# ScalarE's copies of the turned probabilities, moved ahead of a weight slot's high part in the attention steps

## The chip, the cores and the metric

The kernel runs on one core of one Trainium2 chip. The metric is the device time of one execution in microseconds (us), as a median over runs. Five engines of the core have instruction streams of their own: TensorE (PE in the profile, with PEld for its weight loads), VectorE (DVE), ScalarE (ACT), GpSimd (POOL) and SyncE (SP), which issues the weight transfers. Each stream is written out by hand, and semaphores tie them together.

## What is computed

Two transformer stacks run one after the other on one sequence of 256 tokens and width 1024, with float32 inputs. The change lies in the first stack, whose two layers each do this, cut to what matters:

```python
h = h + 0.5 * swiglu(rmsnorm(h, g0), ...)            # d_ff 2816
u = rmsnorm(h, g1)
cols = u @ w_in[l]                                   # projections of four mixers
y_a = mla_mixer(...)    # 8 heads, dense causal
y_b = swa_mixer(...)    # 8 heads, window 128, with sinks
y_c = nsa_mixer(...)    # 8 heads: compressed, selected and window attention
y_d = diff_mixer(...)   # 4 heads, difference of two softmaxes
merged = sum(sigmoid(u @ w_gate[l, b]) * (y_b_ @ w_branch[l, b]) for b in range(4))
h = h + merged @ w_o[l]
h = h + 0.5 * swiglu(rmsnorm(h, g2), ...)
```

The second stack (dilated attention, then retention, each between two feed-forward blocks) is not touched.

## The kernel before, in words

**Weights.** All weights come as a stream of slots of 128x3072 float32 (1.5 MB) into a ring in SBUF. A product of full precision is made from two parts of each operand, a high part (the value rounded to fp32r) and a low part (the rest). For a slot, ScalarE writes the high part (`take_high`, line L1579, tile `ring_hi`, two buffers), VectorE subtracts it from the slot to get the low part (`take_low`, L1961, tile `ring_lo`), and TensorE then multiplies with both. `take_high` waits until the slot has landed (`weights_in`) and until TensorE has done with the slot that last used the same `ring_hi` buffer (`ring_used`).

**The attention of a layer** is one loop of 22 steps on every engine, `for t in range(STEPS)`. It does three things interleaved: the softmax attention of 20 pairs of heads, the small compression network of the third mixer (`compress`), and the projections and gated merges that fill TensorE's time. In step t TensorE does, in this order:

- `scores(t)`: the scores of pair t (banks 0 and 1 of PSUM);
- `turn(t)`: it transposes the probabilities of pair t-1 into banks 2 and 3 (L1175; six matmuls for a pair of two jobs, three in steps 9 to 12, whose pairs are differential heads with one job);
- two pieces, number 2t and 2t+1: a projection `tile` for numbers below 12, and a `merge` from number 12 (step 6) on. A merge multiplies a gate's weights (24 matmuls) and, for most, a branch's (12 matmuls) from the slot of that step;
- `values(t-1)`: the turned probabilities of pair t-1 times the values.

A merge writes into one of two PSUM banks, and so waits until VectorE has emptied the bank of the merge two numbers before (semaphore `merged`, in `merge`, by `merge_emptied`).

**VectorE** does in step t: `empty(2t-1)` (scales the gate of piece 2t-1 into `gate_in`, L2601), `bias_max(t)` (L2507 to L2513), `add(2t-1)` (`add_branch`: L2616 for the first branch, L2618 and L2620 for the others; it waits for ScalarE's tanh of the gate), `take_low` of the slot, `normalise(t)` (L2523 to L2542), `empty(2t)`, `low_outputs`, `compress(t)`, `add(2t)`. Within it, step 3 gives `cmp_kv_out` (L2461), for which TensorE's `turn(4)` waits; step 5 gives `cmp_shifted` (L2478), for which `turn(6)` waits; the end of step 14 is `low_diff` of step 14 (L2566), for which `turn(15)` waits.

**ScalarE** does in step t: `compress(t)`, `take_high` of the slot, `copy_pT(t-1)` (L1846: it copies the turned probabilities from banks 2 and 3 to SBUF, once for each job, and waits for TensorE's `turn(t)` by `probs_turned`), the tanh of gate 2t-1 (`gate`, L1851), `exps(t)` (L1834, L1835), `copy_outputs` (L1860), and the tanh of gate 2t. Every step's slot is listed in `SPLIT_STEPS` (steps 0, 2, 3 and 5 to 20). In steps 0, 2 and 20 (`LATE_SPLITS`) `take_high` stands behind `exps`; in the other 16 it stands where the change is.

The three streams share no scheduler: the order of the calls in the source is the order on the engine.

Of the kernel before, what the change touches and what calls it, by code (L numbers as in the profile page):

```python
# [174 lines left out]
def build(nc, stream, x_rows, norm_gT_2, gains_2, table_2, pick_2, ret_const, decay, norm_gT, mla_gT, sinks, posT, lam, subln, table_1, consts, flip_dram, pick_1, out):  # L175

    ctx = ExitStack()
    with ctx:
# [309 lines left out]
        def mix_slot(l):  # L488
            return l * C_LAYER + C_FFN
# [102 lines left out]
        PAIRS = NU // 2  # L592

        def jobs(t):

            return 1 if UNITS[2 * t]["kind"] == "diff" else 2
# [3 lines left out]
        def jobs_before(l, t):  # L600

            return l * JOBS_LAYER + sum(jobs(n) for n in range(t))
# [99 lines left out]
        def merge_at(i):  # L702

            return i - 12 if i >= 12 else None
# [18 lines left out]
        def branches_before(m):  # L723

            return sum(merge_parts(n)[3] for n in range(m))
# [54 lines left out]
        def emptied_before(c):  # L780


            return SPLIT_SLOTS[SPLIT_INDEX[c] - 2] + 1
# [788 lines left out]
        def _(act):  # L1572

            def take_high(c):

                act.wait_ge(weights_in[c % NS], 16 * (c // NS + 1))
                if SPLIT_INDEX[c] >= 2:
                    act.wait_ge(ring_used, emptied_before(c))
                act.activation(split_part(c, high(c)), split_part(c, ring[:, c % NS, :]), ACT.Copy)\  # L1579
                    .then_inc(hi_ready, 1)  # L1580
# [75 lines left out]
            def take_high_late(c):  # L1656


                act.wait_ge(weights_in[c % NS], 16 * (c // NS + 1))
                act.activation(high(c)[:, 0:2 * D], ring[:, c % NS, 0:2 * D], ACT.Copy).then_inc(hi_ready, 1)  # L1660

            def take_high_unused(c):


                act.wait_ge(weights_in[c % NS], 16 * (c // NS + 1))
                act.activation(high(c)[:, 2 * D:], ring[:, c % NS, 2 * D:], ACT.Copy).then_inc(hi_back, 1)
# [151 lines left out]
            def compress(l, t):  # L1818
                if t == 3:
                    act.wait_ge(cmp_taken, 2 * l + 2)  # L1820
                    act.activation(hidC[:, :, :], hidC[:, :, :], ACT.Gelu_apprx_tanh).then_inc(cmp_gelu, 1)
                elif t == 6:
                    act.wait_ge(cmp_shifted, l + 1)
                    act.activation(ce[:, :, :, :], cs[:, :, :, :], ACT.Exp).then_inc(cmp_exp, 1)

            def exps(l, t):
                if t or l:
                    act.wait_ge(probs_turned, jobs_before(l, t))
                s = pair_soft(l, t)
                for j, u in enumerate(UNITS[2 * t:2 * t + 2]):  # L1830
                    a = l * NU + 2 * t + j
                    x, p = biased_sb[:, j, :], probs_sb[:, j, :]
                    act.wait_ge(negmax_ready, a + 1)
                    act.activation(p[:, 0:P], x[:, 0:P], ACT.Exp, bias=s[:, 1, j, 0:1], accum_out=s[:, 2, j, 0:1])  # L1834
                    last = act.activation(p[:, P:3 * P], x[:, P:3 * P], ACT.Exp, bias=s[:, 1, j, 1:2],  # L1835
                                          accum_out=s[:, 2, j, 1:2])
                    if u["kind"] == "swa":
                        last = act.activation(s[:, 3, j, :], s[:, 1, j, :], ACT.Exp, bias=sink[:, l, u["head"]:u["head"] + 1])
                    last.then_inc(exp_done, 1)

            def copy_pT(l, t):
                for j in range(jobs(t)):
                    act.wait_ge(probs_turned, jobs_before(l, t) + j + 1)
                    if l or t:
                        act.wait_ge(attn_out, jobs_before(l, t))
                    act.activation(pT_sb[:, j, :], ps[:, 2 + j, 0:3 * P], ACT.Copy).then_inc(pT_ready, 1)  # L1846

            def gate(l, m):
                g = gates_before(m)
                act.wait_ge(gate_scaled, 32 * l + g + 1)  # L1850
                act.activation(gate_place(m), gate_in[:, g % 2, :], ACT.Tanh, scale=0.5).then_inc(sig_ready, 1)  # L1851

            def copy_outputs(l, t):


                if branch_copy(t) is None:
                    return
                dst, src = branch_copy(t)
                act.wait_ge(attn_out, jobs_before(l, t + 1))
                act.activation(dst.rearrange("p f t -> p (f t)"), src, ACT.Copy).then_inc(branch_in, 1)  # L1860

            def copy_diff(l):
                for fp in range(2):
                    act.wait_ge(diff_turned, 2 * l + fp + 1)
                    act.activation(yT[0][:, 2 * fp:2 * fp + 2, :].rearrange("p f t -> p (f t)"), ps[:, 2 + fp, :],
                                   ACT.Copy).then_inc(branch_in, 1)

            def attention(l):
                for t in range(STEPS):
                    compress(l, t)  # L1870
                    if t in SPLIT_STEPS and t not in LATE_SPLITS:
                        take_high(mix_slot(l) + SPLIT_STEPS[t])
                    if 1 <= t <= PAIRS:
                        copy_pT(l, t - 1)
                    if t and merge_at(2 * t - 1) is not None:
                        gate(l, merge_at(2 * t - 1))
                    if t < PAIRS:
                        exps(l, t)
                    if t in SPLIT_STEPS and t in LATE_SPLITS:
                        take_high(mix_slot(l) + SPLIT_STEPS[t])  # L1880
                    if t >= 2:
                        copy_outputs(l, t - 2)
                    if t == 14:
                        copy_diff(l)
                    if merge_at(2 * t) is not None:
                        gate(l, merge_at(2 * t))
                gate(l, merge_at(2 * STEPS - 1))
                take_high(mix_slot(l) + S_BRANCH_2 + 1)
                take_high_unused(mix_slot(l) + S_WO)
                for k in range(K_SPLIT):  # L1890
                    if k == 3:
                        act.wait_ge(ring_used, emptied_before(mix_slot(l) + S_WO))
                        take_high_late(mix_slot(l) + S_WO)
                    act.wait_ge(merged, 32 * l + branches_before(32) + 1 + k)
                    act.activation(mTh[:, k, :], mT[:, k, :], ACT.Copy).then_inc(merged_hi, 1)
                take_high(mix_slot(l) + S_WO + 1)
# [8 lines left out]
            for l in range(DEPTH):  # L1905
                norm(3 * l + 0, norm_g[:, l, 0, :])
                ffn(2 * l, layer_slot(l))
                take_high_late(layer_slot(l) + C_FFN + 1)
                take_high_back(layer_slot(l) + C_FFN)
                norm(3 * l + 1, norm_g[:, l, 1, :])  # L1910
                take_high_back(layer_slot(l) + C_FFN + 1)
                act.wait_ge(r_ready, 3 * l + 2)
                projections(l)
                attention(l)
                for j in range(2):
                    take_high(layer_slot(l + 1) - C_FFN + j)
                norm(3 * l + 2, norm_g[:, l, 2, :])
                ffn(2 * l + 1, layer_slot(l + 1) - C_FFN)
                take_high_late(layer_slot(l + 1) + 1)
# [1080 lines left out]
```

## Time and profile before

| | |
|---|---|
| median of 3 runs | 2782.04 us (2781.07 to 2783.23) |
| the profiled execution | 2783.28 us, its span 2781.2 us |
| PE busy | 2733.8 us, 98% of the span |
| PEld busy | 2399.6 us, 86% |
| DVE busy | 1879.8 us, 68% |
| ACT busy | 1387.9 us, 50% |
| steps 1 to 21 of the attention, first layer | 292 to 514 us of the span |
| the same, second layer | 1003 to 1225 us |

Busy time counts an engine's instructions; an engine that waits on a semaphore isn't busy. A wait is shown in brackets behind a row of the timeline: how long the engine sat idle before the instruction, and what released it. The second layer's attention repeats the first's 711.3 us later, row for row, with differences of a few tenths.

### The profile page before, as it was taken

To read this page: it belongs to the slowest core of one execution; us is meant where nothing else is said; L and a number is where in the kernel's file an instruction comes from. 1 tells how busy PE (TensorE), PEld (TensorE's weight loads), DVE (VectorE), ACT (ScalarE), POOL (GpSimd) and SP (SyncE) were. 2 spreads that over 40 slices of the span, in tenths; PEclk is the share of its full clock that TensorE was granted. 3 is DMA by queue.
4 is the path that set the end of the run, shared out by engine and by line. 5 is a ranking of instruction groups with operands and counts; after the bars stand their busy time and mean duration, and the time that the engine had idled before them with its cause. 6 is when DMAs were issued, how large, how long until landed. Compare 5 with 4: busy or idle time off the path is not lost.

```text
span 2781.2 us, 42124 instructions
## 1 busy us (share of the span) xinstructions
PE 2733.8 (98%) x16902; PEld 2399.6 (86%) x16902; DVE 1879.8 (68%) x2840; ACT 1387.9 (50%) x1960; POOL 103.0 (4%) x131
## 2 busy tenths in 40 slices
PE   8999999999999999999999999999999999999998
PEld 7888999888888989988888889997888889987787
DVE  6676678666776657867676675555667666755766
ACT  5453455454545545545455454445455454453554
POOL 1000000000000000001001001110000000000000
PEclk9999999999999999999999999999999999999999
DMA  7554343445455543446455545453454455444453
GB/s 265 187 203 160 142 155 137 182 170 192 177 185 183 203 160 139 158 159 236 183 183 192 190 179 172 166 178 133 181 191 171 181 191 190 163 150 168 159 184 125
DMA packets 49670, 488.46 MB, mean 176 GB/s; under 512 B 6656, under 2 KB 6864, under 8 KB 11272
## 3 DMA queue, kind: packets, MB, share of 16 engines
q1 hardware_dynamic: 44200, 471.71, 45.9%
q0 software_dynamic: 5344, 14.98, 1.9%
q8 instruction: 90, 1.47, 0.2%
q14 instruction: 36, 0.29, 0.0%
HBM read 485.47 MB, written 1.19 MB: 175 GB/s over the span
## 4 chain that ended last, share of the span: by engine, by line
PE 91%; DVE 5%; ACT 1%; issue 1%; DMA 0%; POOL 0%; SPq 0%; DVEq 0%; ACTq 0%
PE ps L896 70%; PE ps L961 17%; DVE ring_lo L1961 2%; PE ps L912 1%; PE ps L1175 1%; ACT ring_hi L1579 1%; PE ps L1385 1%; PE ps L1400 1%; DVE xn L2108 0%; PE ps L1292 0%; DVE work_all L2618 0%; DVE uT L1985 0%; PE ps L1027 0%; PE ps L1082 0%; PE ps L924 0%
## 5 line engine op out<-in xcount | busy, mean ns | idle before, releaser
L896 PE MATMUL ps<-uT,ring_hi 128*128 128x512 f32 (+1 forms) x5536 | 1509.6, 344 | 4.2 <-DVE ring_lo L1989 2.6
L896 PE MATMUL ps<-uT,ring_lo 128*128 128x256 f32 x4176 | 1176.7, 282 | 0.0
L896 PEld LDWEIGHTS ps<-uT,ring_hi 128*128 128x128 f32 x5536 | 954.9, 190 | 138.7 <-DVE ring_lo L1989 3.0
L896 PEld LDWEIGHTS ps<-uT,ring_lo 128*128 128x128 f32 x4176 | 794.5, 190 | 6.2
L2074 DVE TENSOR_TENSOR ring_lo<-ring,ring_hi 128x2048 fp32r<-128x2048 f32 x160 | 366.8, 2293 | 221.1 <-ACT ring_hi L1647 221.1
L1961 DVE TENSOR_TENSOR ring_lo<-ring,ring_hi 128x3072 fp32r<-128x3072 f32 (+1 forms) x110 | 352.0, 3200 | 140.4 <-ACT ring_hi L1579 140.1
L1579 ACT ACTIVATE ring_hi<-ring 128x3072 fp32r<-128x3072 f32 (+1 forms) x110 | 290.8, 2644 | 210.0 <-PE ps L896 198.6
L1647 ACT ACTIVATE ring_hi<-ring 128x2048 fp32r<-128x2048 f32 x160 | 304.1, 1901 | 0.0
L961 PE MATMUL ps<-ring_hi,hid_hi 128*128 128x512 f32 x704 | 276.3, 392 | 0.0
L961 PE MATMUL ps<-ring_lo,hid_hi 128*128 128x512 f32 x704 | 276.1, 392 | 0.0
L961 PE MATMUL ps<-ring_hi,hid_lo 128*128 128x512 f32 x704 | 274.2, 389 | 0.0
L896 PE MATMUL ps<-ring_hi,uT 128*128 128x384 f32 (+1 forms) x1024 | 259.2, 333 | 0.2
L1637 ACT ACTIVATE work_all<-ps 128x512 f32<-128x512 f32 x168 | 100.4, 598 | 309.0 <-PE ps L896 308.3
L1640 ACT ACTIVATE work_all<-work_all 128x256 f32<-128x256 f32 x168 | 70.2, 418 | 299.6 <-DVE work_all L2062 299.6
L2025 DVE TENSOR_TENSOR ring_lo<-ring,ring_hi 128x1024 fp32r<-128x1024 f32 x176 | 214.6, 1219 | 4.2 <-ACT ring_hi L1620 4.2
L896 PEld LDWEIGHTS ps<-ring_hi,uT 128*128 128x128 f32 x1024 | 183.4, 188 | 1.2 <-issue 1.1
L1620 ACT ACTIVATE ring_hi<-ring 128x1024 fp32r<-128x1024 f32 x176 | 183.9, 1045 | 0.0
L896 PE MATMUL ps<-ring_lo,uT 128*128 128x384 f32 (+1 forms) x512 | 169.3, 331 | 0.0
L961 PEld LDWEIGHTS ps<-ring_hi,hid_hi 128*128 128x128 f32 x704 | 132.2, 188 | 31.9 <-DVE hid_lo L2069 1.2
L961 PEld LDWEIGHTS ps<-ring_hi,hid_lo 128*128 128x128 f32 x704 | 132.3, 188 | 29.1
L961 PEld LDWEIGHTS ps<-ring_lo,hid_hi 128*128 128x128 f32 x704 | 132.2, 188 | 21.0
L2059 DVE TENSOR_TENSOR work_all<-ps,work_all 128x512 f32<-128x512 f32 x168 | 115.8, 689 | 38.4 <-ACT work_all L1637 38.1
(317 smaller groups left out, 2805.3 us busy)
## 6 DMA issues: line engine op xcount, KB each, us to landing
ring<-stream_dram SPq DMA_DIRECT2D x297, 1536.0 KB, 6.3
mlaT_all<-bias_vectors POOLq DMA_DIRECT2D x32, 96.0 KB, 2.8
bias<-gains_dram POOLq DMA_DIRECT2D x5, 512.0 KB, 7.7
ring<-stream_dram SPq DMA_DIRECT2D x4, 512.0 KB, 7.7
yR<-bias_vectors POOLq DMA_DIRECT2D x1, 2048.0 KB, 13.9
mlaT_all<-bias_vectors POOLq DMA_DIRECT2D x32, 64.0 KB, 3.3
row<-ret_const_dram POOLq DMA_DIRECT2D x1, 1280.0 KB, 5.8
h<-x_rows_dram SPq DMA_DIRECT2D x2, 512.0 KB, 4.7
```

The source lines that it names most:

```text
L896: m = pe.matmul(out_, lhsT, rhs, start=start, stop=stop, **kw)
L912: last = pe.transpose(ps[:, banks[kp], j * SEQ + tt * P:j * SEQ + tt * P + P], h[:, tt, k * P:(k + 1) * P], ident)
L961: last = pe.matmul(ps[:, n, :], x, w[:, cols], start=False, stop=final and x is x_lo, skip_group_check=True)
L1579: act.activation(split_part(c, high(c)), split_part(c, ring[:, c % NS, :]), ACT.Copy)\
L1620: act.activation(high(c)[:, 2 * D:3 * D], ring[:, c % NS, 2 * D:3 * D], ACT.Copy).then_inc(down_hi, 1)
L1637: act.activation(gu_low, ps[:, 4 + 2 * (g % 2):6 + 2 * (g % 2), SEQ:2 * SEQ], ACT.Copy)\
L1640: act.activation(sil[:, g % 2, :], gu[:, g % 2, 0, :], ACT.Silu).then_inc(silu_ready, 1)
L1647: act.activation(high(c)[:, 0:2 * D], ring[:, c % NS, 0:2 * D], ACT.Copy).then_inc(hi_ready, 1)
L1961: dve.tensor_tensor(split_part(c, ring_lo[:, c % NS, :]), split_part(c, ring[:, c % NS, :]), split_part(c, high(c).bitcast(F32)), ALU.subt ...
L2025: dve.tensor_tensor(ring_lo[:, c % NS, 2 * D:3 * D], ring[:, c % NS, 2 * D:3 * D], high(c)[:, 2 * D:3 * D].bitcast(F32), ALU.subtract)
L2059: dve.tensor_tensor(gu[:, g % 2, :, :], ps[:, 4 + 2 * (g % 2):6 + 2 * (g % 2), 0:SEQ], gu_low, ALU.add).then_inc(gu_summed, 1)
L2074: dve.tensor_tensor(ring_lo[:, c % NS, 0:2 * D], ring[:, c % NS, 0:2 * D], high(c)[:, 0:2 * D].bitcast(F32), ALU.subtract).then_inc(lo_rea ...
```

## The change

In ScalarE's stream, in each step of the attention, `copy_pT(l, t - 1)` is now called ahead of `take_high`. Nothing is added or removed, and the streams of the other engines are the same.

```diff
             def attention(l):
                 for t in range(STEPS):
                     compress(l, t)
+                    if 1 <= t <= PAIRS:
+                        copy_pT(l, t - 1)
                     if t in SPLIT_STEPS and t not in LATE_SPLITS:
                         take_high(mix_slot(l) + SPLIT_STEPS[t])
-                    if 1 <= t <= PAIRS:
-                        copy_pT(l, t - 1)
                     if t and merge_at(2 * t - 1) is not None:
                         gate(l, merge_at(2 * t - 1))
```

The order changes in steps 3 and 5 to 19 of each layer, 16 steps. On ScalarE, before, from the tanh of gate 30 (end of step 15) to the tanh of gate 32 (end of step 16); L1579 is the slot's high part, L1846 the copies, L1851 a tanh:

```order
L1851 ACTIVATE gate_out<-gate_in 128x256 [waits gate_scaled]
L1579 ACTIVATE ring_hi<-ring 128x3072 [waits ring_used,weights_in_3]
L1846 ACTIVATE work_all<-ps 128x384 [waits attn_out,probs_turned] x2
L1851 ACTIVATE gate_out<-gate_in 128x256 [waits gate_scaled]
L1834 ACTIVATE work_all,soft<-xn,soft 128x128 [waits negmax_ready,probs_turned]
L1835 ACTIVATE work_all,soft<-xn,soft 128x256
L1834 ACTIVATE work_all,soft<-xn,soft 128x128 [waits negmax_ready]
```

The same piece in the changed kernel:

```order
L1851 ACTIVATE gate_out<-gate_in 128x256 [waits gate_scaled]
L1846 ACTIVATE work_all<-ps 128x384 [waits attn_out,probs_turned] x2
L1579 ACTIVATE ring_hi<-ring 128x3072 [waits ring_used,weights_in_3]
L1851 ACTIVATE gate_out<-gate_in 128x256 [waits gate_scaled]
L1834 ACTIVATE work_all,soft<-xn,soft 128x128 [waits negmax_ready,probs_turned]
L1835 ACTIVATE work_all,soft<-xn,soft 128x256
L1834 ACTIVATE work_all,soft<-xn,soft 128x128 [waits negmax_ready]
```

The two copies with their wait for `probs_turned` have passed the high part; the tanh and the exponentials stand behind both, as they did.

On ScalarE, before, in step 3, behind the Gelu of the compression network (L1821):

```order
L1821 ACTIVATE yR<-yR 128x60 [waits cmp_taken]
L1579 ACTIVATE ring_hi<-ring 128x3072 [waits ring_used,weights_in_3]
L1846 ACTIVATE work_all<-ps 128x384 [waits attn_out,probs_turned] x2
L1834 ACT_TABLE_LOAD [waits negmax_ready]
L1834 ACTIVATE work_all,soft<-xn,soft 128x128 [waits probs_turned]
```

and in the changed kernel:

```order
L1821 ACTIVATE yR<-yR 128x60 [waits cmp_taken]
L1846 ACTIVATE work_all<-ps 128x384 [waits attn_out,probs_turned] x2
L1579 ACTIVATE ring_hi<-ring 128x3072 [waits ring_used,weights_in_3]
L1834 ACT_TABLE_LOAD [waits negmax_ready]
L1834 ACTIVATE work_all,soft<-xn,soft 128x128 [waits probs_turned]
```

Here too only the two rows have changed places.

## Rows read from the trace of the kernel before

**Rows 1.** Busy time by stretches: us, busy us (instructions) of PE, PEld, DVE, ACT, POOL, clock
```profile
420.00:500.00 80.00, 78.92 (x662) 72.48 (x661) 64.26 (x168) 43.90 (x97) 1.64 (x1) 1.00 0.37 139
```

**Rows 2.** Timeline, step 17: start, duration, engine, line, instruction, [idle before, releaser]
```profile
465.02 2.77 ACT L1579 ACTIVATE ring_hi<-ring 128x3072 fp32r<-128x3072 f32 x1 [0.93 <-PE ps L896]
465.93 0.88 PE L1175 MATMUL ps<-cst,work_all 128*128 128x128 f32 x6
466.57 0.48 PE L896 MATMUL ps<-uT,ring_hi 128*128 128x256 f32 x2
467.69 0.85 ACT L1846 ACTIVATE work_all<-ps 128x384 f32<-128x384 f32 x2
468.43 0.42 ACT L1851 ACTIVATE gate_out<-gate_in 128x256 f32<-128x256 f32 x1
469.33 0.42 DVE L2620 TENSOR_TENSOR mlaT_all<-mlaT_all,work_all 128x256 f32<-128x256 f32 x1
470.94 0.40 PE L896 MATMUL ps<-uT,ring_hi 128*128 128x256 f32 x2
```

**Rows 3.** Timeline, ACT and PE, step 14: copies that wait for their turn
```profile
434.22 0.87 PE L1175 MATMUL ps<-cst,work_all 128*128 128x128 f32 x6
434.81 0.87 ACT L1846 ACTIVATE work_all<-ps 128x384 f32<-128x384 f32 x2 [0.60 <-PE ps L1175]
```

**Rows 4.** Timeline, PE and DVE, step 19: a merge that waits for its bank
```profile
488.05 0.88 PE L1175 MATMUL ps<-cst,work_all 128*128 128x128 f32 x6
491.74 0.42 DVE L2620 TENSOR_TENSOR mlaT_all<-mlaT_all,work_all 128x256 f32<-128x256 f32 x1
492.22 0.51 PE L896 MATMUL ps<-uT,ring_hi 128*128 128x256 f32 x2 [0.42 <-DVE mlaT_all L2620]
```

**Rows 5.** Timeline, step 3 and the turn of step 4
```profile
318.12 0.82 PE L1175 MATMUL ps<-cst,work_all 128*128 128x128 f32 x6
323.15 0.18 DVE L2523 RECIPROCAL soft<-soft 128x4 f32<-128x4 f32 x1 [0.35 <-ACT work_all L1835]
325.05 0.27 DVE L2461 COPY yR<-ps 15x128 f32<-15x128 f32 x1
326.93 0.88 PE L1175 MATMUL ps<-cst,work_all 128*128 128x128 f32 x6
```

**Rows 6.** Timeline, step 5 and the turn of step 6
```profile
336.31 0.87 ACT L1846 ACTIVATE work_all<-ps 128x384 f32<-128x384 f32 x2 [2.06 <-PE ps L1175]
337.45 3.35 DVE L1961 TENSOR_TENSOR ring_lo<-ring,ring_hi 128x3072 fp32r<-128x3072 f32 x1
343.78 0.41 DVE L2478 TENSOR_TENSOR yR<-yR 128x240 f32<-128x240 f32 x1
346.04 0.87 PE L1175 MATMUL ps<-cst,work_all 128*128 128x128 f32 x6
```

**Rows 7.** Timeline, end of step 7 on DVE and the turn of step 8
```profile
367.62 0.41 DVE L2616 SCALAR_TENSOR_TENSOR mlaT_all<-gate_out,ps 128x256 f32<-128x256 f32 x1
368.15 0.88 PE L1175 MATMUL ps<-cst,work_all 128*128 128x128 f32 x6
```

**Rows 8.** Timeline, step 11 and the first merge of step 12
```profile
400.54 0.55 PE L1175 MATMUL ps<-cst,work_all 128*128 128x128 f32 x3
402.44 0.41 ACT L1851 ACTIVATE gate_out<-gate_in 128x256 f32<-128x256 f32 x1
410.02 0.42 DVE L2620 TENSOR_TENSOR mlaT_all<-mlaT_all,work_all 128x256 f32<-128x256 f32 x1
411.35 0.48 PE L896 MATMUL ps<-uT,ring_hi 128*128 128x256 f32 x2
```

**Rows 9.** Timeline, DVE in step 14 and the turn of step 15
```profile
437.48 0.42 DVE L2620 TENSOR_TENSOR mlaT_all<-mlaT_all,work_all 128x256 f32<-128x256 f32 x1
443.82 0.44 PE L1175 MATMUL ps<-cst,work_all 128*128 128x128 f32 x2 [0.46 <-DVE xn_r L2566]
```

**Rows 10.** Waits, PE, whole span: who waited <- for whom, us in all, times, longest
```profile
PE ps L896 <- DVE mlaT_all L2620: 1.3, 3, 0.4
```

## The prediction

> **What bounds the kernel now.** I read the busy times first. In a stretch of the attention TensorE is busy 78.92 of 80 us, VectorE 64.26 and ScalarE 43.90 [rows 1]. TensorE sets the time, and whatever the change does must show as more or less waiting on TensorE. The waits of TensorE there are few and short: 0.42 us for a merge's bank in step 19 [rows 4], one of three such in the whole span [rows 10], 0.46 us at the turn of step 15 [rows 9]. So hardly anything can be gained on TensorE in these steps, some 1 us a layer. What can be lost is decided by how early VectorE's results arrive, and this I read from the timeline of single steps. Step 17 stands for them [rows 2]. TensorE's turn of the probabilities starts at 465.93, the first merge at 466.57, which is 0.64 behind the turn's start, and the second merge at 470.94, which is 5.01 behind it. That second merge needs the bank that VectorE empties in `add(2t-1)`, whose last row (L2620) ends at 469.33 + 0.42 = 469.75: 1.19 us of spare time. That add had followed the tanh of the gate, which starts at 468.43 on ScalarE, and ends 1.32 behind its start.
>
> **What the change does to one step.** In step 17 the slot's high part starts at 465.02, when the slot before is released, 0.91 us *ahead* of the turn, and the copies find their data ready when it is done [rows 2]. With the copies ahead, ScalarE has to wait for the turn first. How fast the copies follow a turn is seen where they waited for one: 434.81 - 434.22 = 0.59 behind its start [rows 3]. The two copies take 468.43 - 467.69 = 0.74, one copy half of that, 0.37, and the high part 467.69 - 465.02 = 2.67 [rows 2]. So the tanh starts 0.59 + 0.74 + 2.67 = 4.00 behind the turn's start where two jobs are copied, and 3.63 behind where one is. In step 17 it is 2.50 before: everything behind it on ScalarE (the tanh, the exponentials, `copy_outputs`) comes 1.50 later. VectorE had waited for that tanh, so it too slips by 1.50, with all it does until the next step: the low part, `normalise`, the gate of piece 2t, `low_outputs`, `compress`, the next add. The copies themselves come 1.2 earlier, and nobody gains: TensorE needs them for `values`, at the end of the step.
>
> **Where TensorE then waits,** in the first layer. From VectorE's end to TensorE's start I take 0.06 us: in step 19 VectorE's row ends at 491.74 + 0.42 = 492.16, and TensorE starts at 492.22 [rows 4]. Time lost at one place moves TensorE's later rows too, so each term is what comes on top.
>
> - Steps 16, 17, 18: the pair of the add ends 4.00 + 1.32 = 5.32 behind the turn's start, TensorE can start at 5.38 and wants to at 5.01 [rows 2]: 0.37 each, 1.11.
> - Step 19: its second merge has a gate only behind it and came at 492.22, after a wait of 0.42 for the same thing [rows 4]. Now 488.05 + 5.38 = 493.43: 1.21 more.
> - Steps 10 and 11 (one job): in step 11 the tanh moves from 402.44 to 400.54 + 3.63 = 404.17, by 1.73. The add at the step's end, whose last row ends at 410.44, ends at 412.17. The merge that needs it starts at 411.35 now, and would at 412.23 [rows 8]: 0.88 for the two steps, as step 10 leaves about half of it.
> - Step 7: the slip of 1.50 reaches the end of VectorE's step, which is unbroken work since the compression network falls in it. Its last add ends at 368.03 + 1.50 = 369.53, and TensorE wants its bank 0.64 behind the turn at 368.15, at 368.79 [rows 7]: 0.80.
> - Step 14: the pair of the add ended at 437.90 and would at 434.22 + 5.32 = 439.54 [rows 3, 9]: 1.64. Behind it VectorE works without a break up to the result for which the turn of step 15 waits already, by 0.46 [rows 9]. So all 1.64 is lost.
> - Step 3: the copies start at 318.12 + 0.59 = 318.71, the high part at 319.45, and ends 2.76 later at 322.21; the low part takes 3.27 and ends at about 325.5, where `normalise` now starts at 323.15: a slip of 2.35. The copy that the turn of step 4 waits for ends at 325.32 now, then at 327.67, and the turn was at 326.93 [rows 5]: 0.80.
> - Step 5: the copies stay at 336.31, the high part comes behind them at 337.05 and ends at 339.82, and the low part starts there, not at 337.45: a slip of 2.37. The row for which the turn of step 6 waits ends at 344.19, then 346.56, and the turn was at 346.04 [rows 6]: 0.58.
> - Steps 6, 8, 9, 12, 13, 15: the same working leaves between 0.1 and 1 us of spare time. I cost them at nothing; the cover is thinnest in steps 8 and 9, about 0.1 us.
>
> The sum is 1.11 + 1.21 + 0.88 + 0.80 + 1.64 + 0.80 + 0.58 = 7.02 us a layer. The second layer repeats it, so 14.0 us. The profiled execution was 2783.28 us with a span of 2781.2, 1.24 above the median of 2782.04; the sum goes on either alike, and on the median it gives **2796.1 us**, 0.5% slower. From below the terms are bounded by those two that meet a wait already there, 1.64 and 1.21 in each layer: 5.7 us, 2787.7. From above, I take every term as good for half as much again and 0.3 us more in each of six covered steps of a layer: 21.1 + 3.6 = 24.7, 2806.7. I take the middle working, since each of its terms rests on a row of its own place.
>
> **A rule that speaks for no loss.** In these steps ScalarE is busy only 43.90 of 80 us [rows 1], yet VectorE waits for it. The Trainium skill (Perfetto Trace Analysis, Identifying the Most-Contended Engine) takes the engine with the highest occupancy for the one to work on, and for ScalarE takes occupancy as a fair measure. Read as a rule of cost, it would give 2782: an engine half idle has room for a reordering. The rows speak against that reading: step 19 has TensorE waiting on a chain that runs through it [rows 4]. The same page, further on, says to look for the semaphore behind each gap, and that is what the sum does.
>
> **The rivals.**
>
> *Spare time swallows it (not slower).* The place is the bank of the second merge. If the add's pair comes before 5.01 behind the turn, that is if the slip is under 1.13 us and not 1.50, steps 10, 11 and 16 to 18 cost nothing; if the copies followed the turn's first transposes more closely and the slips in steps 3, 5, 7, 14 and 19 were taken up as well, the time would stay at 2782. For it: ScalarE idles 36 of 80 us. Against it: the two waits that are there already leave no room at their places. Price 0, at most 5 us: 2782 to 2787.
>
> *ScalarE's chain becomes the loop.* If a slip isn't caught up within its step, because VectorE starts the next step late and hands that on, each of the 16 steps would pay its 1.50: 16 x 1.50 x 2 = 48 us, 2830. Against it: VectorE is busy 64.26 of 80 us [rows 1], which leaves it about 2 us in a step of 11, more than the slip; and where a chain starts from TensorE's own turn, as here, a wait of TensorE moves the start of the next chain as well and isn't paid twice.
>
> *Faster.* Should the earlier copies release anything on TensorE, only its present waits there could go, about 1 us a layer: 2780. Nothing on TensorE waits for a copy of the probabilities in these steps. That the change does nothing can be left out: ScalarE's order differs in 16 steps of each layer, and in step 17 the turn is later than the slot's release.
>
> **How the numbers follow.** A difference of 0.2%, 5.6 us, is about what a measurement of this kernel can tell from none. The forecast, with misses of single terms, 2790 to 2803: 0.70. Spare time swallows it: 0.10, and 0.03 more for results between. More handed on from step to step than I have, 2803 to 2812: 0.11. The loop, 2830: 0.04. Faster: 0.02. The range 2788 to 2808 leaves out the swallowed case, the loop, the faster case and some of the results above. Slower by over 0.2% holds 0.70 + 0.11 + 0.04 and a third of the between: 0.86. Within 0.2%: 0.12. Faster: 0.02.
>
> **What the profile of the changed kernel would show.** In each of the 16 steps the copies stand ahead of the high part with a wait for TensorE's turn (in step 17 of about 2.2 us more idle time than the high part had), and the tanh 4.00 behind the turn's start. Among TensorE's waits, L896 for VectorE's L2620 rises from 1.3 us in all [rows 10] to some 7 or more, and new ones come at the turns of steps 4 and 6, for L2461 and L2478. The turn of step 15 waits longer than 0.46, in part ahead of it at the second merge of step 14. The attention of each layer is 7 us longer, and nothing outside it changes. I am wrong if the tanh is 4.00 behind the turn and TensorE still doesn't wait (there is another buffer or another order than I read), or if TensorE waits for the low part of a slot, L1961, which I have as ready 1 us or more ahead.

## The result, and the profile after

| | before | after |
|---|---|---|
| median | 2781.56 us (2780.17 to 2783.23, 4 runs) | 2800.76 us (2799.53 to 2802.23, 4 runs) |
| the profiled execution | 2783.28 us | 2800.34 us |
| its span | 2781.2 us | 2798.2 us |

The changed kernel is slower: 1.0065 times the time of before, with a 95% interval of 1.0053 to 1.0077. The medians lie 19.2 us apart. The prediction was 2796.1 us with a range of 2788 to 2808.

The page of the profile shows no work that is new. The span and the busy times of the changed kernel:

```profile
span 2798.2 us, 42124 instructions
PE 2736.3 (98%) x16902; PEld 2397.5 (86%) x16902; DVE 1878.3 (67%) x2840; ACT 1387.0 (50%) x1960; POOL 103.1 (4%) x131
```

Busy time is within 3 us of before on every engine. The 17.0 us of the span are waiting, and the same stretch that [rows 1] shows has less work in it now (columns as there):

```profile
420.00:500.00 80.00, 76.91 (x639) 70.31 (x637) 62.77 (x165) 41.01 (x90) 1.64 (x1) 1.00 0.37 138
```

TensorE is busy 76.91 of 80 us where it was 78.92, at the same granted clock of 1.00. What it waits for is in its list of waits over the whole span (who waited <- for whom, us in all, times, longest):

```profile
PE ps L896 <- DVE mlaT_all L2620: 7.6, 16, 1.6
...
PE ps L896 <- DVE mlaT_r L2566: 2.3, 2, 1.1
PE ps L896 <- DVE ring_lo L1961: 2.2, 3, 0.8
PE ps L1175 <- DVE xn_r L2566: 2.1, 2, 1.1
...
PE ps L1175 <- DVE yR L2461: 1.4, 2, 0.7
...
PE ps L1175 <- DVE yR L2478: 1.1, 2, 0.6
PE ps L896 <- DVE mlaT_all L2616: 1.1, 2, 0.5
```

The first of them answers to [rows 10], 1.3 us in 3 waits. The second is the one that I had not forecast. The third, for a slot's low part, stood in the list of before with the same 2.2 us in 3 waits: the low parts still come in time.

**Step 17,** which answers to [rows 2], in time order over the three engines:

```profile
472.56 0.88 PE L1175 MATMUL ps<-cst,work_all 128*128 128x128 f32 x6
473.15 0.88 ACT L1846 ACTIVATE work_all<-ps 128x384 f32<-128x384 f32 x2 [1.41 <-PE ps L1175]
473.90 2.77 ACT L1579 ACTIVATE ring_hi<-ring 128x3072 fp32r<-128x3072 f32 x1
476.56 0.42 ACT L1851 ACTIVATE gate_out<-gate_in 128x256 f32<-128x256 f32 x1
477.01 0.42 DVE L2618 SCALAR_TENSOR_TENSOR work_all<-gate_out,ps 128x256 f32<-128x256 f32 x1 [2.47 <-ACT gate_out L1851]
477.47 0.43 DVE L2620 TENSOR_TENSOR mlaT_all<-mlaT_all,work_all 128x256 f32<-128x256 f32 x1
477.95 0.51 PE L896 MATMUL ps<-uT,ring_hi 128*128 128x256 f32 x2 [0.21 <-DVE mlaT_all L2620]
484.10 0.88 PE L1175 MATMUL ps<-cst,work_all 128*128 128x128 f32 x6
```

It is read downward as one chain. TensorE's turn starts at 472.56. The copies follow 0.59 behind it, the high part at 473.90, the tanh at 476.56, exactly 4.00 behind the turn. VectorE had stood idle for 2.47 us for that tanh, empties the bank by 477.90, and TensorE's second merge starts at 477.95, 5.39 behind the turn, where it stood 5.01 behind it in [rows 2]. The bracket shows only 0.21 us of these 0.38, since it counts from the end of the matmul before, and before the change that matmul still ran for 0.17 us when the second merge started. The next turn comes 11.54 behind this one; it was 11.06 (465.93 to 476.99).

**The turns as a ruler.** From the starts of L1175 in the two timelines, each step can be charged with what it added. Only intervals between turns that changed by more than 0.03 us are in the table, in us; the forecast is that of the prediction's term.

| interval between turns | before | after | more | the term it answers to | forecast |
|---|---|---|---|---|---|
| 3 to 4 | 8.81 | 9.57 | 0.76 | step 3 | 0.80 |
| 5 to 6 | 10.31 | 10.93 | 0.62 | step 5 | 0.58 |
| 8 to 9 | 11.28 | 12.09 | 0.81 | step 7 | 0.80 |
| 9 to 10 | 10.61 | 11.99 | 1.38 | step 9 | 0 |
| 11 to 12, 12 to 13 | 10.50 each | 10.98 each | 0.96 | steps 10 and 11 | 0.88 |
| 14 to 15 | 9.60 | 11.24 | 1.64 | step 14 | 1.64 |
| 16 to 17, 17 to 18, 18 to 19 | 11.06 each | 11.54 each | 1.44 | steps 16 to 18 | 1.11 |
| 19 to 20 | 8.31 | 9.53 | 1.22 | step 19 | 1.21 |

That makes 8.83 us in the first layer, and 0.1 us in intervals of 0.01 or 0.02. In the second layer the other lines are the same within 0.02 us; 14 to 15 grew from 9.32 to 11.25 (1.93) and 19 to 20 from 8.02 to 9.53 (1.51), 9.5 us in all. So the two attentions cost 18.4 us.

**The interval that was missed,** 9 to 10, by its rows in the changed kernel:

```profile
385.20 0.41 ACT L1851 ACTIVATE gate_out<-gate_in 128x256 f32<-128x256 f32 x1
385.64 0.42 DVE L2616 SCALAR_TENSOR_TENSOR mlaT_all<-gate_out,ps 128x256 f32<-128x256 f32 x1 [2.32 <-ACT gate_out L1851]
391.30 0.42 DVE L2566 TENSOR_TENSOR mlaT_r<-ps,yR_r 128x256 fp32r<-128x256 f32 x1
391.87 0.91 PE L896 MATMUL ps<-row,work_all 128*128 128x128 f32 x6 [1.14 <-DVE mlaT_r L2566]
```

and the same place in the kernel before, from its timeline:

```profile
387.66 0.42 DVE L2566 TENSOR_TENSOR mlaT_r<-ps,yR_r 128x256 fp32r<-128x256 f32 x1
...
388.43 0.83 PE L896 MATMUL ps<-row,work_all 128*128 128x128 f32 x6
```

Before, VectorE's row ended at 388.08 and TensorE took up `values(8)` at 388.43, without a bracket: 0.35 us lie between the two. The turn of step 9 was at 379.43 before and is at 381.57 now. Counted from it, the row's end went from 8.65 to 10.15, by the 1.50 of the prediction, and TensorE's start from 9.00 to 10.30. In the source, `values` of step 9 is the first of the differential heads'. It writes into banks of PSUM from which VectorE must first have taken the outputs of the last pair before, in `low_outputs` (L2566) of the same step. The pairs before it (2 to 7) wait for the same semaphore, but for the `low_outputs` of one step earlier, and those behind it (9 to 11) don't wait for it at all:

```python
if two[0]["kind"] == "diff":
    if t == 8:
        pe.wait_ge(branch_low, copied + 8)
```

**Behind the attentions** the distance between the two records isn't constant. It is 18.3 us at turn 20 of the second layer (1225.37 - 1207.07) and 17.0 at the end. At one norm between the two, windows of 1 us in the kernel before read:

```profile
1641.00:1642.00 1.00, 1.00 (x7) 1.00 (x6) 0.53 (x1) 0.62 (x2) 0.00 (x0) 0.50 0.35 98
1642.00:1643.00 1.00, 1.00 (x6) 1.00 (x6) 0.42 (x1) 1.00 (x4) 0.00 (x0) 0.50 0.78 172
```

and at the same norm in the changed kernel:

```profile
1659.00:1660.00 1.00, 0.77 (x7) 0.53 (x6) 0.80 (x2) 0.88 (x3) 0.00 (x0) 1.00 0.09 25
1660.00:1661.00 1.00, 0.95 (x8) 0.71 (x7) 0.56 (x1) 1.00 (x3) 0.00 (x0) 1.00 0.99 233
```

The granted clock is 0.50 in the one and 1.00 in the other, after a wait of TensorE of 2.9 us for VectorE in both. The matmuls of this norm took 3.30 us before (1640.26 to 1643.56) and 2.71 now (1658.53 to 1661.24). This is a difference between two records, not an effect that I can tie to the change: the medians lie 19.2 us apart, above the 18.4 of the attentions. TensorE waits for 2.6 to 4.1 us at six norms behind the attentions, and in eleven of these twelve places of the two records its clock is at 0.50 for some us afterwards; only the norm shown from the changed kernel keeps 1.00. The half clock sets in at different moments, too: the norm at 1448.18 before runs its first eight matmuls at 1.00, and in the changed kernel, where it starts at 1466.48, the window 1466:1467 is at 0.55 already. The distance is still 18.3 us at the start of the norm shown, and 16.9 at the start of the last one (2599.05 - 2582.17).

### The profile page after: what moved, and what is told of

It reads as the page before. It is cut to its first block, busy times and chain, and to the rows that moved or that the text cites. A ratio compares the mean times of both kernels' runs of the same rounds, so it can differ in the third digit from the quotient of the medians.

```text
span 2798.2 us, 42124 instructions
## 1 busy us (share of the span) xinstructions
PE 2736.3 (98%) x16902; PEld 2397.5 (86%) x16902; DVE 1878.3 (67%) x2840; ACT 1387.0 (50%) x1960; POOL 103.1 (4%) x131
## 3 DMA queue, kind: packets, MB, share of 16 engines
HBM read 485.47 MB, written 1.19 MB: 174 GB/s over the span
## 4 chain that ended last, share of the span: by engine, by line
PE 88%; DVE 6%; ACT 3%; issue 2%; DMA 0%; POOL 0%; SPq 0%; DVEq 0%; ACTq 0%
PE ps L896 67%; PE ps L961 17%; DVE ring_lo L1961 2%; ACT ring_hi L1579 2%; PE ps L1175 1%; PE ps L912 1%; PE ps L1385 1%; PE ps L1400 1%; DVE xn L2108 0%; DVE uT L1985 0%; DVE work_all L2618 0%; PE ps L1292 0%; DVE mlaT_all L2620 0%; POOL r_tok L2747 0%; PE ps L1027 0%
## 5 line engine op out<-in xcount | busy, mean ns | idle before, releaser
L1961 DVE TENSOR_TENSOR ring_lo<-ring,ring_hi 128x3072 fp32r<-128x3072 f32 (+1 forms) x110 | 352.0, 3200 | 156.2 <-ACT ring_hi L1579 155.9
L1579 ACT ACTIVATE ring_hi<-ring 128x3072 fp32r<-128x3072 f32 (+1 forms) x110 | 290.8, 2644 | 182.7 <-PE ps L896 171.4
```

Of the source, the lines that this page charges most:

```text
L1961: dve.tensor_tensor(split_part(c, ring_lo[:, c % NS, :]), split_part(c, ring[:, c % NS, :]), split_part(c, high(c).bitcast(F32)), ALU.subt ...
```

## The experiments

All kernels here compute the whole of the output. In those that change only some steps, a condition in the loop adds three lines to the source, so that L2566, L2616 and L2620 read L2569, L2619 and L2623. The times of before are those of runs on the same chip: 2783.14 us for the first four kernels, 2782.16 us for the last four. The kernels with the change in step 9, in (14, 19), in (6, 8, 12, 13, 15), in (3, 5, 7) and the one with an extra copy were run once each. Single runs of before spread over 2780.0 to 2785.0 us, so the time of these five says little; what they show is read from the intervals between turns.

**Which part of the loss is step 9's.** Two kernels: the change in step 9 alone, and everywhere but there.

```diff
+                    copies_first = t == 9
+                    if 1 <= t <= PAIRS and copies_first:
+                        copy_pT(l, t - 1)
                     if t in SPLIT_STEPS and t not in LATE_SPLITS:
                         take_high(mix_slot(l) + SPLIT_STEPS[t])
-                    if 1 <= t <= PAIRS:
+                    if 1 <= t <= PAIRS and not copies_first:
                         copy_pT(l, t - 1)
```

> The copies stand ahead of the high part in step 9 of each layer alone; all other steps are as in the kernel before. Theory (the wait that the prediction didn't have): in step 9 VectorE's tail slips by 1.5 us, with it the low part of the last MLA/SWA outputs (L2566), for which TensorE's first differential values (L896, row,work_all) wait. TensorE's turn of step 10 comes 1.38 us later than in the kernel before, counted from the turn of step 9, with a new wait of about 1.1 us on L2566, in each layer; span +2.8 us. Rival (the wait in step 9 is what steps 7 and 8 hand on): with those steps as before, the turn of step 10 comes at most 0.4 us later, and no wait on L2566 stands there; span +0 to +0.8 us.

It ran in 2784.23 us with a span of 2782.1. The interval from turn 9 to 10 is 11.98 us in both layers, 1.37 more, and no other interval moved. TensorE's list of waits has one line more than before:

```profile
PE ps L896 <- DVE mlaT_r L2569: 2.3, 2, 1.1
```

The same 2.3 us, twice 1.1, as in the changed kernel. Nothing was handed on from steps 7 or 8, since those are as before here: the loss is step 9's own.

The other kernel has `t != 9` for the condition.

> The change in 15 steps of each layer, without step 9. Theory (each step's debt is its own): from the turn of step 9 to that of step 10 it is 10.6 us again as in the kernel before, not 12.0, all other steps take what they take in the changed kernel; 2.8 us a run less than the changed kernel, 15 to 16 us above the kernel before, ratio 1.0055. Rival (a debt that isn't paid in step 9 is paid in step 10 or 11): the steps behind it take longer by about 1.4 us in all, ratio 1.0065 as the changed kernel.

It ran in 2798.02 us, 1.0055 times before (1.0038 to 1.0072). Its turn 9 to 10 is back at 10.61 us, and every other interval is that of the changed kernel within 0.02. At the turns the two parts together make the whole within 0.1 us.

**The two places with a wait already there.** With `t in (14, 19)` for the condition:

> The copies stand ahead in steps 14 and 19 of each layer alone, the two dearest terms of the sum. Theory: the turn of step 15 comes 1.64 us later and that of step 20 another 1.22 us, in the first layer; a few tenths more in the second, where the waits before are shorter; span +5.7 to 6.2 us. Rival (ScalarE's chain hands its slip from step to step): both steps follow punctual ones, so each costs less than in the changed kernel, together under 4 us for both layers.

It ran in 2788.45 us with a span of 2786.3. Turn 14 to 15 is 11.24 us and turn 19 to 20 is 9.53 in the first layer, 11.25 and 9.52 in the second: the same as in the changed kernel, all other intervals as before. That is 6.3 us at the turns, and 5.3 in the time of this one run. The rows of step 14:

```profile
439.80 0.51 PE L896 MATMUL ps<-uT,ring_hi 128*128 128x256 f32 x2 [0.76 <-DVE mlaT_all L2623]
445.66 0.87 PE L1175 MATMUL ps<-cst,work_all 128*128 128x128 f32 x6 [1.07 <-DVE xn_r L2569]
```

The slip is paid in two places, 0.76 us at the second merge and 1.07 at the turn of step 15, for which TensorE waited 0.46 in [rows 9]. So it is right to count it once, at the turn.

**The steps costed at nothing,** without step 9: `t in (6, 8, 12, 13, 15)`.

> The copies stand ahead in steps 6, 8, 12, 13 and 15 of each layer alone, which the prediction costs at nothing. Theory: ScalarE's tanh comes 1.5 us and more later in them, VectorE's tail with it, and TensorE's turns stay where they are, within 0.1 us a layer; span within 0.3 us of before. Rival (every slip is paid): 5 x 1.5 x 2 = 15 us longer.

It ran in 2785.51 us with a span of 2783.4, and the theory fell in part. Step 6 is free with a slip of 1.50 us, step 8 costs 0.03. Step 15 is free too, but it tests nothing: its high part started behind the turn before the change as well, and the tanh is 4.02 us behind the turn in both kernels. But turn 12 to 13 is 10.98 us, 0.48 more, and turn 14 to 15 is 11.02, 1.42 more. The rows:

```profile
411.81 0.55 PE L1175 MATMUL ps<-cst,work_all 128*128 128x128 f32 x3
416.81 0.50 PE L896 MATMUL ps<-uT,ring_hi 128*128 128x256 f32 x2 [0.20 <-DVE mlaT_all L2623]
...
440.63 0.51 PE L896 MATMUL ps<-uT,ring_hi 128*128 128x256 f32 x2 [0.54 <-DVE mlaT_all L2623]
446.49 0.87 PE L1175 MATMUL ps<-cst,work_all 128*128 128x128 f32 x6 [1.06 <-DVE xn_r L2569]
```

In step 12 the second merge waits 0.20 us, and starts 5.00 behind the turn. In step 14, whose own order is that of before, the slip of step 13 comes through: VectorE is 1.42 us late at its end. In the full change the two cost nothing more. There TensorE has waited in step 12 already at the first merge, for step 11's slip, and in step 14 the slip of 1.64 that starts from the turn is the later of two arrivals. One wait covers the other; they don't add up. For steps 13 and 14 the run with (14, 19) shows it, with the same 11.24 us without step 13's slip; for steps 11 and 12 it is read from the rows of the changed kernel, where the second merge of step 12 comes 5.08 behind the turn without a wait of its own.

**The three early steps:** `t in (3, 5, 7)`. I ran it since the interval 8 to 9 could have been the slip of step 8 instead of 7.

> The copies stand ahead in steps 3, 5 and 7 of each layer alone. Theory: TensorE's turns of steps 4 and 6 come 0.77 and 0.62 us late, waiting on L2461 and L2478 of VectorE, and the turn of step 9 another 0.81, since the first merge of step 8 waits for the last add of step 7; 2.2 us a layer, span +4.4 us. Rival (step 8's own slip makes the 0.81): 1.4 us a layer, +2.8 us.

It ran in 2788.98 us with a span of 2786.9. Turn 3 to 4 is 9.58 us, 5 to 6 is 10.93 and 8 to 9 is 12.08 with step 8 unchanged. TensorE's waits for it:

```profile
PE ps L1175 <- DVE yR L2464: 1.4, 2, 0.7
...
PE ps L1175 <- DVE yR L2481: 1.1, 2, 0.6
PE ps L896 <- DVE mlaT_all L2619: 1.1, 2, 0.6
```

These are the three lines for L2461, L2478 and L2616 of the changed kernel, with the same sums. Each term of these steps stands by itself, 2.2 us a layer. The time of this one run lies 6.8 us above that of before, where the turns account for 4.5; its turn of step 2 already comes 1.35 us later than in the record of before, ahead of all changed steps.

**What in the order costs: the copies or the tanh?** If the loss comes through the tanh, as the prediction has it, then a tanh ahead of the high part should bring much of it back, with the copies still first.

```diff
                     compress(l, t)
-                    if t in SPLIT_STEPS and t not in LATE_SPLITS:
-                        take_high(mix_slot(l) + SPLIT_STEPS[t])
                     if 1 <= t <= PAIRS:
                         copy_pT(l, t - 1)
                     if t and merge_at(2 * t - 1) is not None:
                         gate(l, merge_at(2 * t - 1))
+                    if t in SPLIT_STEPS and t not in LATE_SPLITS:
+                        take_high(mix_slot(l) + SPLIT_STEPS[t])
```

> As the changed kernel, but the tanh of gate 2t-1 is called ahead of the high part too: copies, tanh, high part. Theory (the debts of steps 10, 11 and 16 to 19 run through the tanh, those of steps 3, 5, 7, 9 and 14 through the high part and the low part behind it): the tanh starts 1.3 us behind the turn, the waits on L2620 at second merges go, steps 16 to 18 take 11.06 us again, steps 10 and 11 at most 0.2 us too much each; steps 3 and 5 keep their 0.77 and 0.62, steps 7, 9 and 14 keep about 0.5, 0.9 and 0.9, step 19 about 0.4 to 0.7. Sum 4 to 5 us a layer, ratio 1.003. Rival (any delay of the high part costs TensorE what it is late): high part still 1.5 to 2 us late in all, so ratio 1.0055 to 1.0065.

It ran in 2793.95 us, 1.0044 times before (1.0029 to 1.0059): a third of the loss is gone, where 1.003 was expected. At the turns in the first layer: steps 16 to 18 cost 0 where they cost 0.48 each, step 19 costs 0.42 instead of 1.22, step 9 costs 1.05 instead of 1.38. Steps 3 and 5, where the copies and the high part alone are at play, stay at 0.77 and 0.63. The interval 11 to 12 costs 0.12 instead of 0.48, and 12 to 13 nothing. So in steps 10, 11 and 16 to 18 the tanh carried it, and in step 19 the larger part of it; in 3 and 5 it was the high part itself. What is left in step 19 comes by the high part too: VectorE waits 1.77 us for it, and the turn of step 20 waits 1.31 us for VectorE's probabilities (L2542). Step 14 is the miss of this run: 1.55 us where 0.9 was expected. Its rows on ScalarE:

```profile
437.57 0.87 ACT L1846 ACTIVATE work_all<-ps 128x384 f32<-128x384 f32 x2 [2.36 <-PE ps L1175]
439.03 0.42 ACT L1851 ACTIVATE gate_out<-gate_in 128x256 f32<-128x256 f32 x1 [0.59 <-DVE gate_in L2601]
439.35 2.75 ACT L1579 ACTIVATE ring_hi<-ring 128x3072 fp32r<-128x3072 f32 x1
```

The tanh now reaches the head of the stream before VectorE has scaled the gate, waits 0.59 us for it, and the high part stands behind that wait too. It starts at 439.35, 2.36 behind the turn, where before the change it started 2.78 us ahead of it (431.44, turn at 434.22). It is what the change does too: a row with a late condition stands ahead of one whose condition is met. The second layer lost 7.1 us, not the 5.0 of the first: 1.55 of it is a stretch at half the clock in step 15, shown at the end.

**And with the tanh ahead of the copies,** the high part first:

```diff
                     if t in SPLIT_STEPS and t not in LATE_SPLITS:
                         take_high(mix_slot(l) + SPLIT_STEPS[t])
-                    if 1 <= t <= PAIRS:
-                        copy_pT(l, t - 1)
                     if t and merge_at(2 * t - 1) is not None:
                         gate(l, merge_at(2 * t - 1))
+                    if 1 <= t <= PAIRS:
+                        copy_pT(l, t - 1)
```

> As the kernel before, but the tanh of gate 2t-1 is called ahead of the copies: high part, tanh, copies, the opposite move. Theory: the tanh comes 0.74 us earlier in steps 16 to 19, VectorE's tail with it, the wait of 0.42 at the second merge of step 19 and that of 0.20 at the turn of step 20 go; the wait of 0.46 at the turn of step 15 stays, as in step 14 VectorE scales the gate late and the tanh can't start before 435.3. About 0.7 us less in the first layer and 0.4 in the second, 1.1 us or 0.04%, seen in the trace alone. Rival (the later copies cost TensorE at its values): over 1 us more.

It ran in 2780.32 us (2779.90 to 2782.63, 11 runs) beside 2782.16: 0.9995 times before, with an interval of 0.9986 to 1.0004. In the trace it is better. Turn 19 to 20 is 7.55 us (before 8.31) in the first layer and 7.36 (8.02) in the second, 1.4 us together, and all other intervals are as before. Step 19 on ScalarE:

```profile
487.94 2.77 ACT L1579 ACTIVATE ring_hi<-ring 128x3072 fp32r<-128x3072 f32 x1 [1.98 <-PE ps L896]
490.61 0.40 ACT L1851 ACTIVATE gate_out<-gate_in 128x256 f32<-128x256 f32 x1
490.92 0.85 ACT L1846 ACTIVATE work_all<-ps 128x384 f32<-128x384 f32 x2
```

The tanh is 2.04 us behind its turn of 488.57. The wait of 0.42 us of [rows 4] is gone, and so is one of 0.2 at the turn of step 20. The wait of 0.46 us at the turn of step 15 stays, as expected. A measurement of the whole kernel doesn't tell 1.4 us from none.

**The price of a microsecond on this chain.** The changed kernel, with a copy of 128x256 from PSUM to a tile that nothing reads, ahead of the high part in steps 16 to 18 of the first layer; the second layer is the control.

```diff
                     act.activation(pT_sb[:, j, :], ps[:, 2 + j, 0:3 * P], ACT.Copy).then_inc(pT_ready, 1)
+                if l == 0 and t in (15, 16, 17):
+                    n = t - 15
+                    act.activation(extra[:, n, :], ps[:, 2, 0:2 * P], ACT.Copy)
```

> The changed kernel with one more ScalarE copy of 128x256 (some 0.33 us from start to start, to a tile that nothing reads) behind the two copies in steps 16, 17 and 18 of the first layer alone; the second layer is the control. Theory (in these steps ScalarE's chain from the turn to the second merge sets the time, and nothing spare is left in it): the turns are 11.54 + 0.33 = 11.87 us apart in the first layer and 11.54 in the second; span +1.0 us. Rival (what makes a step 11.54 is a fixed cost of starting again, or the turn itself): 11.54 in both.

It ran in 2800.91 us. The lines of its source after the new copy stand 4 further down, on TensorE 1. Step 17:

```profile
474.24 0.39 ACT L1850 ACTIVATE extra<-ps 128x256 f32<-128x256 f32 x1
474.50 2.78 ACT L1580 ACTIVATE ring_hi<-ring 128x3072 fp32r<-128x3072 f32 x1
...
478.55 0.50 PE L897 MATMUL ps<-uT,ring_hi 128*128 128x256 f32 x2 [0.48 <-DVE mlaT_all L2624]
```

The copy took 474.50 - 474.24 = 0.26 us from start to start, and not the 0.33 that was expected. TensorE's wait rose from 0.21 to 0.48, by 0.27, and the three intervals are 11.81, 11.82 and 11.81 us, with 11.54 in the second layer: 0.27 more each. Once the spare time of this place is used up (1.19 us less the 0.06 of the hand-over), what comes on top on ScalarE ahead of the tanh comes on top of the kernel's time as well, on an engine that is busy for half of the time. It is shown for this one size.

## Why the prediction was right, and where its sum was short

**The mechanism** held in all steps but one. The copies wait for the turn, the tanh is 4.00 us behind its start with two jobs, and with one job in step 9 it is 385.20 - 381.57 = 3.63. The forecast of that for each of the 16 steps has two exceptions. In step 15 the copies don't wait and nothing slips, since the high part stood behind the turn already. In step 13 the tanh is only 3.16 behind the turn, since the slot's high part is shorter there, but it slips all the same (from 1.42). TensorE waits for L2620 7.6 us (forecast 7 or more), 1.4 and 1.1 us for L2461 and L2478 at the turns of steps 4 and 6, and the turn of step 15 waits longer, in part ahead of it at the second merge. TensorE doesn't wait more for L1961. All of it is VectorE's lateness, none of it TensorE's need of the copies.

**The terms for steps 3, 5, 7, 14 and 19** were met within 0.04 us, steps 10 and 11 within 0.08, in the first layer. The experiments with (3, 5, 7) and (14, 19) alone gave the same numbers without the other steps.

**Step 9, costed at nothing, was the step of the sum that failed:** 1.38 us a layer, 2.8 of the 4.4 us that the turns show above the forecast of 14.0. The slip of 1.50 was known. What I left out is a second reader of VectorE's stream: I had followed merges and turns as the places where TensorE waits, and `values` only for its wait for the copies. In step 9 `values` also waits for `low_outputs` of its own step, with 0.35 us between VectorE's end and TensorE's start. At this place the hand-over alone took 0.15 (391.72 to 391.87), so 0.20 was spare. A slip of 1.50 us over that can't be covered, and it could be read from two rows of the trace of before. "Thinnest in steps 8 and 9, about 0.1 us" was looked for at the wrong wait.

**Steps 16 to 18** were mis-sized by 0.11 us each, 0.48 for 0.37. The merge's start was forecast within 0.01 us (5.39 for 5.38 behind the turn). The rest is in the merge itself: a first pair of matmuls that TensorE doesn't have to wait for takes 0.40 us [rows 2], and one behind a wait 0.51. Step 19 shows the other side of it: it waited before too, its first pair took 0.51 already [rows 4], and its term was right.

**Steps 12 and 13** were costed at nothing, and the sum was right by luck rather than by reading: without the slips of steps 11 and 14 they cost 0.48 and about 1.4 us, and in the full change the waits of steps 11 and 14 cover them. For step 12 the prediction's own sum says it: with one job the add ends 3.63 + 1.32 = 4.95 behind the turn and TensorE could start at 5.01, where in the trace of before its second merge starts at 4.64. So "between 0.1 and 1 us of spare time" was wrong there.

**The second layer doesn't quite repeat the first.** Its turns 14 to 15 and 19 to 20 were 0.28 us shorter than the first layer's before, and end at the same 11.25 and 9.53 us. Where the chain sets the length, both layers have the chain's length; the layer that had less of a wait pays more. That is 0.6 us that a doubling of the first layer's sum can't have.

**One thing that I forecast of ScalarE is wrong,** without a price. The idle time ahead of the copies in step 17 is 1.41 us, 0.48 more than the 0.93 that the high part had, and not 2.2 more. The tanh at the end of the step before ended 1.84 us ahead of the turn and now 0.82, since VectorE's slip isn't wholly taken up by the end of a step.

**The rivals.** Spare time didn't swallow it: the slip is 1.50, over the 1.13 us at which it would have begun. The loop of 2830 us didn't come: steps 6 and 8 slip by 1.50 us and cost 0.03 at most, and with the wait of TensorE the start of the next chain moves as well, as the slope of 1 and no more shows. The Trainium skill (Perfetto Trace Analysis, Identifying the Most-Contended Engine) ranks engines by their occupancy. Read as a rule of cost, as the prediction read it, this case's runs don't bear it out: ScalarE is busy 50% of the span in both kernels (1387.9 and 1387.0 us), and its order costs 19.2 us.

**What is left open.** Between the 18.4 us at the turns and 19.2 in the medians lies less than the interval of either. That the profiled execution has only 17.0 is put down to the clock at the norms behind the attentions, which differs from record to record; no kernel was run to test it.

## What to carry to other kernels

On an engine that works in order, look at each place for the condition that is met last, and keep the rows that wait late behind those that could start at once; how busy the engine is says nothing of it. To cost a slip, list *every* semaphore that the bounding engine takes from the engine that slips, each with its spare time, also those that stand in one step only; a term costed at nothing needs its two rows as much as any other. Where two slips end at the same wait, take the later one and don't add them, and where a new wait is made, add what the restart costs. To see whether a step slips at all, look where its row starts before the change: step 15 was in the list of changed steps and had nothing to lose.

## What the runs showed of the hardware

**A restart has its own price.** The first pair of matmuls of a second merge takes 0.50 or 0.51 us behind a wait and not 0.40, in every such wait for L2620 (brackets of 0.20 to 1.64 us in the traces of these runs), whatever its length. At the first merge of a step, whose first pair follows the turn and takes 0.48 or 0.49 without a wait [rows 2, 8], a wait adds only 0.02 or 0.03.

**The granted clock can fall in the middle of dense work.** In the kernel with the order copies, tanh, high part, the turn of step 15 waited in both layers. In the first:

```profile
448.14 0.87 PE L1175 MATMUL ps<-cst,work_all 128*128 128x128 f32 x6 [1.70 <-DVE xn_r L2566]
```

and the windows behind it have a clock of 1.00. In the second it waited for 1.96 us, and the windows behind it are at half the clock, 1.2 instead of 2.4 GHz:

```profile
1164.51 1.26 PE L1175 MATMUL ps<-cst,work_all 128*128 128x128 f32 x6 [1.96 <-DVE xn_r L2566]
```

```profile
1165.00:1166.00 1.00, 1.00 (x6) 1.00 (x5) 0.97 (x7) 0.85 (x3) 0.00 (x0) 0.50 0.98 418
1166.00:1167.00 1.00, 1.00 (x6) 1.00 (x6) 0.63 (x5) 1.00 (x3) 0.00 (x0) 0.50 0.95 406
```

The step behind it took 12.61 us (1164.51 to 1177.12) and not 11.06, so the wait of 1.96 cost another 1.55. In the changed kernel the clock stayed at 1.00 behind the wait of 1.06 us at the turn of step 15 and behind that of 1.64 in step 19, in both layers. It is one case in one execution, and what decided it isn't shown. Here the wait cost another 0.8 of its own length.
